# The first pair's quarter 12 and the sums s3 and s4 move to GpSimd

## The chip, the cores and the metric

One core of a Trainium2 chip. The metric is the device time of one execution in microseconds (us). Before the change three runs took 2365.22, 2365.63 and 2370.06 us; the median is 2365.63.

## The reference, cut to what matters

One step of a decoder layer for a prompt of 2048 tokens and for 8 samples of 8 tokens, with a model width of 1024. The part that the change touches comes first: the tokens are scaled and shifted by the conditioning vector, and then meet the large input projection.

```python
shift, scale, gate = jnp.split((jax.nn.silu(c) @ w_ada + b_ada)[:, None, :], 3, axis=-1)
h = x * (1 + scale) + shift
proj = h @ w_in
```

Everything that follows (windowed attention, a gated delta rule with its short convolution, two gated branches, an output projection and a layer norm) works on `proj` and is left as it is.

## The kernel before, in words

`modulate_and_project` computes `h` and `proj` with the tokens as the moving operand and the weights, two blocks of 128 output features at a time (a **pair**, counted by q), as the stationary one. There are two passes over the pairs: pass 0 for the first 1024 prompt tokens, pass 1 for the other 1024 and the samples.

Two schemes lie on top of each other. First, seven products stand for eight: the tokens of a pass are cut into four **quarters**, 11, 12, 21 and 22 (the first digit is the half of the tokens, the second the half of the 1024 features; a quarter is 128 partitions by 4 blocks of 512 tokens, so 128x2048), and the products are made of 11, 12, 22 and the sums s1 = 21 + 22, s2 = s1 - 11, s3 = 11 - 21, s4 = 12 - s2, with matching combinations of the weights. Second, each fp32 operand is split in two: a rounded high part (`m_hi` for tokens, `w_hi` for weights, written by ScalarE, line 447 or 423) and a **remainder** (`m_lo`, `w_lo`, written by VectorE as the operand less its high part, line 656 or 627). A product is then three matmuls for each of four blocks of the inner dimension: low by high, high by low, high by high (line 328).

The order of the first pair is written out by hand on each engine, and no planner moves anything:

- **SyncE** issues the loads in one queue: small ones, the first pair's weights, eight blocks of `w_ada`, then the quarters 11, 12, 21 into `x_half` and 22 into `m_sum` (line 243), then small ones and the weights of later pairs.
- **VectorE** (lines 828 to 845) modulates 11 in four pieces as soon as the shift and scale (`mods`, signal `mod_ready`) are there, makes 11's remainder in four pieces (831), modulates 21 (834), makes s3 (662), the remainder of 12 (656), s1, s2, the remainder of s1, s4, and the remainders of s2, 22, s4 and s3. Only then does it take up the results of the pair (`add`, 720) and the next pair's weights (`rest` 627; `weigh`, whose T1 is at line 635).
- **ScalarE** (from line 513) rounds the four pieces of 11 (523), modulates 12 (`modulated`, 439) and rounds it (`rounded`, 447), modulates 22, rounds s3, 22, s1 and s2, copies the first product out of PSUM (`copy_out`, 461), and rounds s4. Then the loop over the pairs starts: it splits the next pair's weights (`split`, 423) between the further copies; the split of form 2 waits for VectorE's T1, and the copy of the fourth product stands behind it.
- **TensorE** (`feature`, `product`) runs the products in the order 11, 12, s1, s2, 22, s4, s3. It waits for the remainder of each; for 11 alone block by block. Before "s2" it also needs the first copy, before "s4" the copy of "s1", and before "s3" that of "s2" (`f2_put`).
- **GpSimd** has no work there: it waits for results to store (lines 945 to 982). Later in the kernel it does have arithmetic: additions and subtractions of two tensors (lines 1612, 2384, 4048 to 4053), one scaling (1351) and memsets.

Of the kernel before, what the change touches and what calls it, by code (L numbers as in the profile page):

```python
# [9 lines left out]
ALU = mybir.AluOpType  # L10
ACT = mybir.ActivationFunctionType
# [4 lines left out]
KT = D // P  # L16
# [36 lines left out]
def f32(ap):  # L53

    return ap.bitcast(F32)
# [15 lines left out]
KH = KT // 2  # L71
PT = SEQ // 2
HT = PT // 2
# [20 lines left out]
def modulate_and_project(nc, t, sc, ab, g_last, head):  # L94
# [3 lines left out]
    with ExitStack() as ctx:  # L98
# [4 lines left out]
        m_hi, m_lo, m_sum = [None] * 7, [None] * 7, [None] * 7  # L103
# [9 lines left out]
        with ExitStack() as early:  # L113
            xs = sb("x_half", [P, 3, KH, WIDE], where=early)
# [29 lines left out]
        mods = sb("ada_mods", [P, 2 * KT, NC])  # L144
# [60 lines left out]
        def tokens(x, s):  # L205

            if s:
                return x[:, :, :]
            return x.rearrange("p k n -> p (k n)")[:, 0:KH * HT].rearrange("p (k n) -> p k n", n=HT)

        def slot(s, m):

            return AHEAD["21" if m == "21v" else m][s]
# [86 lines left out]
        def _(pe):  # L300
# [13 lines left out]
            def product(q, u, j, out, first, start):  # L314
                s = of_pass(q)
                at, n = UNITS[s][u]
                m, x = forms(s)[j]
                if u == 0:
                    pe.wait_ge(w_lo_done[j], q + 1)
                if first and (s, m) != (0, "11"):  # L320
                    pe.wait_ge(m_lo_done[s, m], 1)
                for k in range(KH):
                    if first and (s, m) == (0, "11"):
                        pe.wait_ge(m_lo_done[s, m], k + 1)
                    cols = slice(P * k, P * (k + 1))
                    hi, lo = tokens(m_hi[x], s)[:, k, at:at + n], tokens(m_lo[x], s)[:, k, at:at + n]
                    for nth, (l, r) in enumerate(((wh[j], lo), (wl[j], hi), (wh[j], hi))):
                        last = pe.matmul(out[:, 0:n], l[:, cols], r, start=start and k == 0 and nth == 0, stop=k == KH - 1 and nth == 2,  # L328
                                         skip_group_check=not start)
                last.then_inc(full[j], 1)  # L330
# [83 lines left out]
        def _(act):  # L414
# [18 lines left out]
            def modulated(s, m, x):  # L433
                key = (s, m)
                act.wait_ge(x_in[key], 16 * (1 + s))
                act.wait_ge(mod_ready, 2)
                for k in range(KH):
                    n = KH * (int(m[1]) - 1) + k
                    last = act.activation(x[:, k, 0:HT], x[:, k, 0:HT], ACT.Identity, scale=mods[:, KT + n, 0:1], bias=mods[:, n, 0:1])
                last.then_inc(x_mod[key], 1)  # L440

            def rounded(s, m, x, ready):

                n = HT + SS * s
                for sem_, count in ready:
                    act.wait_ge(sem_, count)
                act.activation(tokens(m_hi[slot(s, m)], s)[:, :, 0:n], x[:, :, 0:n], ACT.Copy).then_inc(m_hi_done[s, m], 1)
# [73 lines left out]
            for k in range(KH):  # L521
                act.wait_ge(x_mod[0, "11"], k + 1)
                act.activation(tokens(m_hi[0], 0)[:, k, :], a11[:, k, 0:HT], ACT.Copy).then_inc(m_hi_done[0, "11"], 1)
            modulated(0, "12", a12), rounded(0, "12", a12, [(x_mod[0, "12"], 1)])
            low = lambda s, m: tokens(m_sum[slot(s, m)], s)
            modulated(0, "22", low(0, "22"))
            rounded(0, "s3", low(0, "s3"), [(sum_put[0, "s3"], 1)])
            rounded(0, "22", low(0, "22"), [(x_mod[0, "22"], 1)])
            for m in ("s1", "s2"):
                rounded(0, m, low(0, m), [(sum_put[0, m], 1)])  # L530
            copy_out(0, 0, 0)
            rounded(0, "s4", low(0, "s4"), [(sum_put[0, "s4"], 1)])
            for q in range(NPAIR):
                nxt = q + 1 < NPAIR
                if q:
# [83 lines left out]
        def _(dve):  # L619
# [31 lines left out]
            def remainder(s, m, x):  # L651

                n = HT + SS * s
                dve.wait_ge(m_hi_done[s, m], 1)
                i = slot(s, m)
                put(dve.tensor_tensor(tokens(m_lo[i], s)[:, :, 0:n], x[:, :, 0:n], f32(tokens(m_hi[i], s)[:, :, 0:n]), ALU.subtract), m_lo_done[s, m])  # L656

            def combine(s, m, out, x, y, op, ready):
                n = HT + SS * s
                for sem_, count in ready:  # L660
                    dve.wait_ge(sem_, count)
                put(dve.tensor_tensor(out[:, :, 0:n], x[:, :, 0:n], y[:, :, 0:n], op), sum_put[s, m])
# [171 lines left out]
                last = dve.tensor_scalar(a21[:, k, 0:HT], a21[:, k, 0:HT], mods[:, KT + k, 0:1], mods[:, k, 0:1], ALU.mult, ALU.add)  # L834
            put(last, x_mod[0, "21"])
            s1, s2, s3, s4 = (low(0, m) for m in ("s1", "s2", "s3", "s4"))
            combine(0, "s3", s3, a11, a21, ALU.subtract, [(x_mod[0, "21"], 1), (x_mod[0, "11"], KH)])
            remainder(0, "12", a12)
            combine(0, "s1", s1, a21, a22, ALU.add, [(x_mod[0, "21"], 1), (x_mod[0, "22"], 1)])
            combine(0, "s2", s2, s1, a11, ALU.subtract, [(sum_put[0, "s1"], 1), (x_mod[0, "11"], KH)])  # L840
            remainder(0, "s1", s1)
            combine(0, "s4", s4, a12, s2, ALU.subtract, [(sum_put[0, "s2"], 1), (x_mod[0, "12"], 1)])
            remainder(0, "s2", s2), remainder(0, "22", a22), remainder(0, "s4", s4), remainder(0, "s3", s3)
            for b in range(4):
                dve.memset(stage[:, b, 0:S_PRE], 0.0)
            for q in range(NPAIR):
# [83 lines left out]
        @block.gpsimd  # L930
        def _(pool):
            def complete(q, j):

                if with_func(q):
                    pool.wait_ge(func_put, func_no(q, j) + 1)
                else:
                    pool.wait_ge((c21, c22)[j], units(q))
                    pool.wait_ge((c11, c12)[j], units(q))

            def store(q):  # L940
                s, n = of_pass(q), SPAN[of_pass(q)]
                dst = t[dict(q="q_d", k="k_T", z="z_d", g="g_d")[kind(q)]]
                for j in range(2):
                    complete(q, j)
                    pool.dma_start(dst[tile(q, j) - 2 * BASE[kind(q)], :, PT * s:PT * s + n],
                                   stage[:, buf(q, j), S_PRE:S_PRE + n]).then_inc(stored[buf(q, j)], 16)

            def store_tail(q):
                for j in range(2):
                    complete(q, j)  # L950
                    pool.dma_start(t["conv_tail"][tile(q, j)], stage[:, buf(q, j), PT:S_W]).then_inc(stored[buf(q, j)], 16)

            def store_conv(q):
                s, n = of_pass(q), SPAN[of_pass(q)]
                for j in range(2):
                    pool.wait_ge(conv_silu, conv_no(q, j) + 1)
                    pool.dma_start(t["conv_d"][tile(q, j), :, PT * s:PT * s + n], conv[:, j, 0:n]).then_inc(conv_stored[j], 16)  # L957

            def store_sums(q):
                s = of_pass(q)  # L960
                for j in range(2):
                    pool.wait_ge(sums_put, norm_pair(q) + 1)
                    row = t["norm_d"][tile(q, j):tile(q, j) + 1]
                    pool.dma_start(row[:, PT * s:PT * (s + 1)].rearrange("a (c n) -> (a c) n", n=HT),
                                   sums[2 * SUB * j:2 * SUB * (j + 1):SUB, :]).then_inc(sums_out, 16)
                    if s:
                        pool.dma_start(row[:, SEQ:], sums_s[SUB * j:SUB * j + 1, :]).then_inc(sums_out, 16)

            def store_all(q):
                if is_conv(q):  # L970
                    if of_pass(q):
                        store_tail(q)
                    store_conv(q)
                    if has_norm(q):
                        store_sums(q)
                else:
                    store(q)
            for q in range(NPAIR):
                store_all(q)
            for v, (s, g, b) in enumerate(VB):  # L980
                pool.wait_ge(v_read[v % 3], v // 3 + 1)
                pool.dma_start(t["v_out"][g, P * b:P * b + v_rows(b), :], v_sb[0:v_rows(b), v % VSLOTS, :]).then_inc(v_stored[v % VSLOTS], 16)
            for q in range(NPAIR, NQ - 1):
                store_all(q)
            for b in range(4):
                pool.wait_ge(stored[b], max(stores_to(q) for q in range(NQ - 1) if 2 * (q % 2) in (b, b - 1)))
            for j in range(2):
                pool.wait_ge(conv_stored[j], 16 * 2 * N_CONV)
            pool.wait_ge(sums_out, 16 * 3 * 2 * NHB)
            for j in range(VSLOTS):  # L990
                pool.wait_ge(v_stored[j], 16 * len(range(j, len(VB), VSLOTS)))
# [3257 lines left out]
```

## Time and profile before

| | us |
|---|---|
| median of three runs | 2365.63 |
| lowest and highest run | 2365.22, 2370.06 |
| the profiled execution, its own time | 2368.39 |
| its span, first to last instruction | 2366.6 |
| TensorE busy | 2255.3 (95% of the span) |
| VectorE busy | 1623.2 (69%) |
| ScalarE busy | 1169.0 (49%) |
| GpSimd busy | 374.4 (16%) |

The profile is of one execution. Times in it count from its first instruction. PE is TensorE's matmuls, PEld its weight loads, DVE is VectorE, ACT ScalarE, POOL GpSimd, SPq SyncE's queue. The mean granted TensorE clock is 0.978 of full speed. A row of an order of time reads: start in us, busy time in us, engine, line, operation, what is written from what is read, shape, number of instructions, and in brackets the idle time of the engine before it and what ended that.

### The profile page before, as it was taken

To read this page: it belongs to the slowest core of one execution; us is meant where nothing else is said; L and a number is where in the kernel's file an instruction comes from. 1 tells how busy PE (TensorE), PEld (TensorE's weight loads), DVE (VectorE), ACT (ScalarE), POOL (GpSimd) and SP (SyncE) were. 2 spreads that over 40 slices of the span, in tenths; PEclk is the share of its full clock that TensorE was granted. 3 is DMA by queue.
4 is the path that set the end of the run, shared out by engine and by line. 5 is a ranking of instruction groups with operands and counts; after the bars stand their busy time and mean duration, and the time that the engine had idled before them with its cause. 6 is when DMAs were issued, how large, how long until landed. Compare 5 with 4: busy or idle time off the path is not lost. (4 is left out here: it accounts for less than half of the span.)

```text
span 2366.6 us, 44948 instructions
## 1 busy us (share of the span) xinstructions
PE 2255.3 (95%) x16842; PEld 2027.6 (86%) x16842; DVE 1623.2 (69%) x3960; ACT 1169.0 (49%) x2457; POOL 374.4 (16%) x627
## 2 busy tenths in 40 slices
PE   5999999999999999999999999969998899999998
PEld 2778788888899999999999978658887689999786
DVE  5877776555363676776655558669986777778797
ACT  4444445444431454444444469647776533333554
POOL 0010100000111011110000001223321035445100
PEclk8999999999999999999999999989999699999999
DMA  7232323332532233223332368976565656666663
GB/s 272 98 116 98 116 99 116 107 107 89 197 116 75 94 105 122 82 109 112 112 109 81 126 235 281 323 218 170 149 185 181 193 172 213 194 206 233 199 208 125
DMA packets 256968, 363.55 MB, mean 154 GB/s; under 512 B 55654, under 2 KB 191438, under 8 KB 252272
## 3 DMA queue, kind: packets, MB, share of 16 engines
q1 hardware_dynamic: 197408, 224.24, 30.7%
q0 software_dynamic: 36496, 124.94, 13.8%
q10 hardware_dynamic: 22848, 11.50, 1.8%
q8 instruction: 134, 2.20, 0.4%
q14 instruction: 82, 0.67, 0.1%
HBM read 246.94 MB, written 113.68 MB: 152 GB/s over the span
## 5 line engine op out<-in xcount | busy, mean ns | idle before, releaser
L328 PE MATMUL ps_f<-m_lo,w_hi 128*128 128x272 f32 (+1 forms) x2436 | 787.8, 323 | 12.5 <-DVE m_lo L656 5.7
L328 PE MATMUL ps_f<-m_hi,w_lo 128*128 128x272 f32 (+1 forms) x2436 | 785.9, 323 | 0.0
L328 PE MATMUL ps_f<-m_hi,w_hi 128*128 128x272 f32 (+1 forms) x2436 | 784.5, 322 | 0.0
L328 PEld LDWEIGHTS ps_f<-m_lo,w_hi 128*128 128x128 f32 x2436 | 459.4, 189 | 52.7 <-issue 16.4
L328 PEld LDWEIGHTS ps_f<-m_hi,w_hi 128*128 128x128 f32 x2436 | 458.7, 188 | 32.2
L328 PEld LDWEIGHTS ps_f<-m_hi,w_lo 128*128 128x128 f32 x2436 | 459.2, 189 | 31.5
L720 DVE TENSOR_TENSOR stage<-partial,ps_f 128x512 f32<-128x512 f32 (+2 forms) x348 | 183.5, 544 | 303.6 <-PE ps_f L328 293.8
L461 ACT ACTIVATE partial<-ps_f 128x272 f32<-128x272 f32 (+1 forms) x348 | 161.2, 463 | 369.7 <-PE ps_f L328 368.7
L423 ACT ACTIVATE w_hi<-w_raw 128x512 fp32r<-128x512 f32 x348 | 213.0, 626 | 190.2 <-PE ps_f L328 110.6
L627 DVE TENSOR_TENSOR w_lo<-w_raw,w_hi 128x512 fp32r<-128x512 f32 x348 | 239.3, 688 | 82.9 <-ACT w_hi L423 78.9
L746 DVE SCALAR_TENSOR_TENSOR conv<-stage,side,conv 128x1024 f32<-128x1024 f32 x108 | 138.3, 1281 | 8.2 <-ACT conv L477 6.9
L66 PE MATMUL ps_f<-wv_lo,m_hi 128*128 128x256 f32 (+1 forms) x384 | 108.9, 284 | 3.7 <-DVE wv_lo L810 3.7
L67 PE MATMUL ps_f<-wv_hi,m_lo 128*128 128x256 f32 (+1 forms) x384 | 109.2, 284 | 0.0
L68 PE MATMUL ps_f<-wv_hi,m_hi 128*128 128x256 f32 (+1 forms) x384 | 108.9, 283 | 0.0
L67 PE MATMUL ps_fm<-u_hi,w_tail_lo 128*128 128x256 f32 (+1 forms) x336 | 95.6, 285 | 0.0
L67 PE MATMUL ps_fm<-u_first_hi,w_tail_lo 128*128 128x256 f32 x336 | 93.0, 277 | 0.0
L1480 ACT ACTIVATE probs<-probs,stats 128x128 f32<-128x128 f32 (+1 forms) x192 | 86.3, 454 | 10.5 <-DVE stats L1451 10.3
L957 POOL DMA_DIRECT2D scratch_conv_d<-conv x36 | 19.5, 540 | 427.5 <-ACT conv L483 420.8
L483 ACT ACTIVATE conv<-conv 128x1024 f32<-128x1024 f32 (+1 forms) x36 | 39.2, 1089 | 81.4 <-DVE conv L746 52.3
L66 PEld LDWEIGHTS ps_f<-wv_lo,m_hi 128*128 128x128 f32 x384 | 73.0, 190 | 4.1 <-DVE wv_lo L810 4.1
L1047 DVE TENSOR_TENSOR sub_prod<-sub_u,sub_w 96x60 f32<-96x60 f32 (+34 forms) x434 | 71.3, 203 | 4.0 <-issue 3.5
L68 PEld LDWEIGHTS ps_f<-wv_hi,m_hi 128*128 128x128 f32 x384 | 73.1, 190 | 0.0
(771 smaller groups left out, 4671.7 us busy)
## 6 DMA issues: line engine op xcount, KB each, us to landing
w_raw<-in_w_feat SPq DMA_DIRECT2D x58, 1024.0 KB, 5.7
gates<-scratch_g_d SPq DMA_DIRECT2D x56, 256.0 KB, 3.4
m_rows<-scratch_parts_d SPq DMA_DIRECT2D x16, 768.0 KB, 4.7
z_f<-scratch_z_d ACTq DMA_DIRECT2D x13, 768.0 KB, 6.8
scratch_conv_d<-conv POOLq DMA_DIRECT2D x18, 544.0 KB, 3.0
scratch_conv_d<-conv POOLq DMA_DIRECT2D x18, 512.0 KB, 2.9
kc<-in_k_cache SPq DMA_DIRECT2D x8, 1152.0 KB, 10.3
vc<-in_v_cache POOLq DMA_DIRECT2D x8, 1152.0 KB, 9.8
```

The lines of the kernel that those rows point to most:

```text
L66: pe.matmul(out, ah, bl, start=start, stop=False)
L67: pe.matmul(out, al, bh, start=False, stop=False)
L68: return pe.matmul(out, ah, bh, start=False, stop=stop)
L328: last = pe.matmul(out[:, 0:n], l[:, cols], r, start=start and k == 0 and nth == 0, stop=k == KH - 1 and nth == 2, skip_group_check=not start)
L423: act.activation(wh[j][:, :], source(q, j), ACT.Copy).then_inc(w_hi_done[j], 1)
L461: act.activation(f[:, which, 0:n], src[:, 0:n], ACT.Copy).then_inc(put, 1)
L483: act.activation(conv[:, j, 0:n], conv[:, j, 0:n], ACT.Silu).then_inc(conv_silu, 1)
L627: put(dve.tensor_tensor(wl[j][:, :], source(q, j), f32(wh[j][:, :]), ALU.subtract), w_lo_done[j])
L720: last = dve.tensor_tensor(by_residue(x[:, S_PRE:S_PRE + PT], stride_of(q), HT * h + at, m), left[:, 0:m], right[:, 0:m], ALU.add)
L746: put(dve.scalar_tensor_tensor(out=conv[:, j, 0:PT], in0=x[:, n:n + PT], scalar=w, in1=conv[:, j, 0:PT], op0=ALU.mult, op1=ALU.add), conv_ ...
L1047: dve.tensor_tensor(prod[:, rows, 0:m], u[:, i:i + 1, i + 1:].broadcast_to(some), w[:, rows, i:i + 1].broadcast_to(some), ALU.mult).then_i ...
L1480: act.activation(own, own, ACT.Exp, scale=-1.0, bias=stats[:, x.g, y.b, head:head + 1], accum_out=stats[:, x.g, y.b:y.b + 1, HPG + head]). ...
```

## The change

In pass 0's first pair, the quarter 12 is modulated by GpSimd, in four pieces that each give a signal, instead of by ScalarE. GpSimd also makes s3 and s4, which VectorE made. ScalarE modulates 22 directly after rounding 11, and then rounds 12 in four pieces, each with its signal; s3 is now rounded behind the first `copy_out`, just ahead of s4. VectorE makes 12's remainder in four pieces, and the remainder of 22 comes ahead of that of s2, with a wait for s4 between. TensorE's product of 12 waits block by block.

```diff
@@ product, TensorE
-                if first and (s, m) != (0, "11"):
+                if first and (s, m) not in ((0, "11"), (0, "12")):
                     pe.wait_ge(m_lo_done[s, m], 1)
                 for k in range(KH):
-                    if first and (s, m) == (0, "11"):
+                    if first and (s, m) in ((0, "11"), (0, "12")):
                         pe.wait_ge(m_lo_done[s, m], k + 1)
@@ ScalarE
-            modulated(0, "12", a12), rounded(0, "12", a12, [(x_mod[0, "12"], 1)])
             low = lambda s, m: tokens(m_sum[slot(s, m)], s)
             modulated(0, "22", low(0, "22"))
-            rounded(0, "s3", low(0, "s3"), [(sum_put[0, "s3"], 1)])
+            for k in range(KH):
+                act.wait_ge(x_mod[0, "12"], k + 1)
+                act.activation(tokens(m_hi[slot(0, "12")], 0)[:, k, :], a12[:, k, 0:HT], ACT.Copy).then_inc(m_hi_done[0, "12"], 1)
             rounded(0, "22", low(0, "22"), [(x_mod[0, "22"], 1)])
             for m in ("s1", "s2"):
                 rounded(0, m, low(0, m), [(sum_put[0, m], 1)])
             copy_out(0, 0, 0)
-            rounded(0, "s4", low(0, "s4"), [(sum_put[0, "s4"], 1)])
+            for m in ("s3", "s4"):
+                rounded(0, m, low(0, m), [(sum_put[0, m], 1)])
@@ VectorE
-            combine(0, "s3", s3, a11, a21, ALU.subtract, [(x_mod[0, "21"], 1), (x_mod[0, "11"], KH)])
-            remainder(0, "12", a12)
+            for k in range(KH):
+                dve.wait_ge(m_hi_done[0, "12"], k + 1)
+                i = slot(0, "12")
+                put(dve.tensor_tensor(tokens(m_lo[i], 0)[:, k, :], a12[:, k, 0:HT], f32(tokens(m_hi[i], 0)[:, k, :]), ALU.subtract), m_lo_done[0, "12"])
             combine(0, "s1", s1, a21, a22, ALU.add, [(x_mod[0, "21"], 1), (x_mod[0, "22"], 1)])
             combine(0, "s2", s2, s1, a11, ALU.subtract, [(sum_put[0, "s1"], 1), (x_mod[0, "11"], KH)])
-            remainder(0, "s1", s1)
-            combine(0, "s4", s4, a12, s2, ALU.subtract, [(sum_put[0, "s2"], 1), (x_mod[0, "12"], 1)])
-            remainder(0, "s2", s2), remainder(0, "22", a22), remainder(0, "s4", s4), remainder(0, "s3", s3)
+            remainder(0, "s1", s1), remainder(0, "22", a22)
+            dve.wait_ge(sum_put[0, "s4"], 1)
+            remainder(0, "s2", s2), remainder(0, "s4", s4), remainder(0, "s3", s3)
@@ GpSimd, ahead of its first store
+            low = lambda m: tokens(m_sum[slot(0, m)], 0)
+            a11, a12, a21 = (xs[:, n, :, 0:HT] for n in (1, 2, 0))
+            pool.wait_ge(x_in[0, "12"], 16)
+            pool.wait_ge(mod_ready, 2)
+            for k in range(KH):
+                n = KH + k
+                pool.tensor_scalar(a12[:, k, :], a12[:, k, :], mods[:, KT + n, 0:1], mods[:, n, 0:1], ALU.mult, ALU.add).then_inc(x_mod[0, "12"], 1)
+            pool.wait_ge(x_mod[0, "11"], KH)
+            pool.wait_ge(x_mod[0, "21"], 1)
+            pool.tensor_tensor(low("s3"), a11, a21, ALU.subtract).then_inc(sum_put[0, "s3"], 1)
+            pool.wait_ge(x_mod[0, "12"], KH)
+            pool.wait_ge(sum_put[0, "s2"], 1)
+            pool.tensor_tensor(low("s4"), a12, low("s2"), ALU.subtract).then_inc(sum_put[0, "s4"], 1)
```

## Rows read from the trace of the kernel before

**Rows 1.** Stretch, length, busy us (count) of PE, PEld, DVE, ACT, POOL; PEclk, DMA share, GB/s.

```profile
66.70:135.00 68.30, 68.26 (x307) 54.34 (x306) 52.81 (x73) 33.25 (x51) 6.70 (x12) 1.00 0.33 120
```

**Rows 2.** TensorE in order of time, the products that begin late, and "s2".

```profile
42.46 0.52 PE L328 MATMUL ps_f<-m_lo,w_hi 128*128 128x512 f32 x1 [2.91 <-DVE m_lo L656]
...
49.78 0.77 PE L328 MATMUL ps_f<-m_lo,w_hi 128*128 128x512 f32 x1 [2.74 <-DVE m_lo L656]
...
54.18 0.47 PE L328 MATMUL ps_f<-m_lo,w_hi 128*128 128x512 f32 x1
...
63.97 0.50 PE L328 MATMUL ps_f<-m_lo,w_hi 128*128 128x512 f32 x1 [1.38 <-ACT partial L461]
```

**Rows 3.** VectorE in order of time, the first pair.

```profile
33.34 2.50 DVE L831 TENSOR_TENSOR m_lo<-x_half,m_hi 128x512 fp32r<-128x512 f32 x4
35.87 1.92 DVE L834 TENSOR_SCALAR x_half<-x_half,ada_mods 128x512 f32<-128x512 f32 x4
...
40.03 2.29 DVE L656 TENSOR_TENSOR m_lo<-x_half,m_hi 128x2048 fp32r<-128x2048 f32 x1
...
51.75 8.89 DVE L656 TENSOR_TENSOR m_lo<-m_sum,m_hi 128x2048 fp32r<-128x2048 f32 x4
...
61.99 0.69 DVE L635 TENSOR_TENSOR w_raw<-w_raw 128x512 f32<-128x512 f32 x1
```

**Rows 4.** ScalarE in order of time: the modulations of 12 and 22, a copy.

```profile
34.20 2.93 ACT L439 ACTIVATE x_half<-x_half,ada_mods 128x512 f32<-128x512 f32 x4
...
38.97 2.93 ACT L439 ACTIVATE m_sum<-m_sum,ada_mods 128x512 f32<-128x512 f32 x4
...
63.33 0.58 ACT L461 ACTIVATE partial<-ps_f 128x512 f32<-128x512 f32 x1
```

**Rows 5.** Token loads: issues (min/median/max ns); issue of 22; us to landing, 12 then 22.

```profile
L243 SPq DMA_DIRECT2D x_half<-in_x_T x3: 448/6767/8660, 7.4 to 14.7; - x3
...
23.41 3.29 SPq L243 DMA_DIRECT2D m_sum<-in_x_T  x1
...
x_half<-in_x_T SPq DMA_DIRECT2D x1, 1024.0 KB, 25.2
...
m_sum<-in_x_T SPq DMA_DIRECT2D x1, 1024.0 KB, 15.3
```

**Rows 6.** GpSimd's arithmetic by line (ns min/median/max, first to last start); its memset.

```profile
L2384 POOL TENSOR_TENSOR ET_first<-G_first,causal_T x12: 1802/1816/1827, 1577.9 to 1737.6; 128x768 f32<-128x768 f32 x12
...
L4048 POOL TENSOR_TENSOR row_sums<-merged x32: 450/476/1442, 1898.3 to 2189.1; 128x128 f32<-128x128 f32 x32
...
L1351 POOL TENSOR_SCALAR q_bd_s<-q_s x12: 359/368/375, 1469.3 to 1473.7; 64x64 f32<-64x64 f32 x12
L1351 POOLq MODIFY_POOL_CONFIG  x2: 8/8/8, 1469.1 to 1469.2; - x2
...
1467.80 1.38 POOL L1344 MEMSET q_bd_s<- 128x1536 f32 x1 [101.25 <-PE ps_s L1380]
```

**Rows 7.** GpSimd and VectorE side by side in order of time; line 1047 by itself.

```profile
1674.25 3.58 POOL L2384 TENSOR_TENSOR ET_first<-G_first,causal_T 128x768 f32<-128x768 f32 x2
...
1676.70 1.18 DVE L1047 TENSOR_TENSOR sub_prod<-sub_u,sub_w 96x31 f32<-96x31 f32 x1
...
L1047 DVE TENSOR_TENSOR sub_prod<-sub_u,sub_w x9: 176/186/1181, 1676.7 to 1680.0; 96x29 f32<-96x29 f32 x2, 96x28 f32<-96x28 f32 x2, 96x31 f32<-96x31 f32 x1, 96x30 f32<-96x30 f32 x1
...
2168.63 0.80 POOL L4053 TENSOR_TENSOR row_sums<-merged,row_sums 128x128 f32<-128x128 f32 x1
2169.02 0.95 DVE L3731 TENSOR_TENSOR w_tail_lo<-x_res,w_hi_ahead 128x512 fp32r<-128x512 f32 x1
...
2169.89 0.68 DVE L3731 TENSOR_TENSOR w_tail_lo<-x_res,w_tail_lo 128x512 fp32r<-128x512 f32 x1
```

**Rows 8.** Busy time by stretch, columns as in the first group: around "s1" and "s2".

```profile
50.00:53.00 3.00, 3.00 (x8) 2.32 (x9) 3.00 (x2) 1.13 (x1) 0.00 (x0) 0.50 0.00 0
53.00:56.00 3.00, 3.00 (x14) 2.27 (x13) 3.00 (x2) 2.31 (x4) 0.00 (x0) 1.00 0.00 0
```

## The prediction

> **What bounds the kernel now.** The view of busy time by stretch comes first [rows 1]: from 66.7 us on TensorE is busy for 68.26 of 68.30 us. So TensorE is the bound behind the first pair, nothing there can win back lost time, and a shift of the first pair's last products goes into the span one for one. The question is only when the seven products of the first pair get their operands.
>
> TensorE's order of time [rows 2] shows where it stood idle: 2.91 us before the product of "12" (42.46), 2.74 us before "s1" (49.78), each until VectorE had a remainder, and 1.38 us before "s3" (63.97), until ScalarE had copied a product out. VectorE's order of time [rows 3] shows that it is the late one: from 33.34 to 60.64 (51.75 + 8.89) it works almost without a gap. A sum or remainder of 128x2048 takes 2.29 us and the next starts 2.2 us after it (8.89 less 2.29, over 3). "s2" started at 54.18, as its remainder came (51.75 + 2.29 = 54.04). From 54.18 to the end of "s4" at 62.59 (63.97 less the idle 1.38) TensorE ran through: 8.41 us for three products. The last wait hangs on VectorE too: ScalarE's copy at 63.33 [rows 4] stands behind the split that needs VectorE's weight difference of 61.99 [rows 3], so it comes 3.3 us (63.33 + 0.58 less 60.64) behind VectorE's last remainder.
>
> **What is removed.** VectorE loses s3 and s4, two instructions, 4.4 us of its chain. ScalarE loses four modulations, 2.93 us [rows 4], and gets four short roundings for a long one. The remainder of 12 becomes four pieces like those of 11, 2.5 us [rows 3] for 2.2: 0.3 more. The new waits on GpSimd stop nothing else of its own: all that is queued behind them there are stores of results of this pair and later ones, and those come after it. No DMA is moved or added, on no queue.
>
> **What is moved on ScalarE.** The modulation of 22 now stands ahead of the rounding of 12. The load of 22 is issued at 23.41 and lands 15.3 us later [rows 5], at 38.7; before, ScalarE came to it at 38.97 and waited for nothing. Now it is free at 34.2, stands until 38.7, modulates until 41.6 (2.93), and only then rounds 12, whose first piece is there at about 42.2. Before, 12's remainder started at 40.03. Passing 12 on in pieces gains nothing if they come this late.
>
> **What GpSimd costs.** The quarter 12 is issued at 7.85 (7.4 and the first issue's 0.45) and lands 25.2 us later [rows 5], at 33.1, so GpSimd starts there. Its two-input operations took 1.81 us for 768 elements and 0.47 for 128 [rows 6]: 2.09 ns for each further element, so some 0.2 fixed, and 4.5 us for the 2048 of s3 or s4, against VectorE's 2.29. Its one-input operation shows only at 64 elements, 0.37 us. For 512 the rows bound it: with the slope to the 1536-element memset (1.38 us, 0.69 ns an element) 0.68 us, with the two-input slope 1.31. I take 0.75, near the lower end, since one input is read.
>
> The first operation of that kind stands 0.1 to 0.2 us behind two MODIFY_POOL_CONFIG [rows 6], so I add nothing for it. The Trainium skill, "GPSIMD Engine Reference", section 2.1, says that the first call to a freshly loaded kernel pays for loading its code, about 6 us, with nothing in the profile to show it. By that the sum would be about 1.9 us longer (the third rival).
>
> **What both engines do to each other** decides. A VectorE operation of 96x31 with both inputs outside PSUM, 0.19 us elsewhere, took 1.18 us at 1676.70 [rows 7]: it ended at 1677.88, just behind the GpSimd pair that ended at 1677.83. So VectorE stands while GpSimd works, for the whole of a long operation. In the other direction GpSimd's 128-element operation took 0.80 between two of VectorE's, and VectorE's next took 0.95 instead of 0.68, 0.27 more, which is 128 times 2.09 ns: they take turns [rows 7]. All of VectorE's sums and remainders here are of that kind. So the 4.4 us taken from VectorE come back as two holds of some 4.4 us and four short ones.
>
> **The sum**, VectorE's chain step by step. The remainders of 11 ended at 35.84; four GpSimd modulations between them, 0.55 each (0.75 less the fixed 0.2), make it 38.0; the modulation of 21 (1.92; its data were there at 35.87 [rows 3]) 40.0. Then s3 runs on GpSimd from 40.1 to 44.6, and 12's first piece, ready at 42.2, waits: it ends the four at 47.1, 4.8 us later than before (42.3). s1 and s2: 51.5. Remainder of s1: 53.7 (before, its product could start at 49.78), its rounding in time at about 51.2. Now s4 has its turn and holds VectorE until 58.1. Remainder of 22: 60.3; of s2: 62.5; of s4: 64.7; of s3: 66.9, which is 6.3 us behind 60.64.
>
> On TensorE "12" starts at about 45.3, "s1" at 53.8, and "s2", whose remainder now stands behind that of 22, at 62.6 instead of 54.18. Three products of 8.41 us in all end at 71.0. The copy for "s3" is there at 66.9 + 3.3 = 70.2, so the 1.38 us of idle time are gone, and "s3" starts at 71.0 instead of 63.97: **7.0 us later**. The clock comes on top: after the idle time before "s1" the granted clock was 0.50 (the 1.2 GHz level) in 50 to 53 us, with 8 matmuls against 14 in the next 3 us at 1.00 (2.4 GHz) [rows 8]. There the slow stretch lay before a wait; now a longer idle time, about 5 us, lies just ahead of "s2", and nothing behind it waits. Six matmuls at 0.227 us (2.72 a product of 12) are 1.4 us. Sum: 8.4 us later.
>
> The profiled execution took 2368.39 us (span 2366.6), so it would be 2376.8. It lies 2.8 us above the median of the runs, 2365.63; on the median the sum gives **2374.0**. A change under 0.2%, 4.7 us, is about what a measurement of this kernel can't tell from none.
>
> **Rivals.** (1) GpSimd holds VectorE up little or not at all over a long operation. Then the remainder of 12 still waits for ScalarE: pieces from 42.2, end at 44.5, s1 and s2 at 48.9, remainder of s1 51.1, of 22 53.4, of s2 55.6 (s4 ready at 53.5). "s2" starts 1.5 us later than before and "s4" ends at 64.1 instead of 62.59, which the 1.38 us of idle time swallow: "s3" starts at about 64.1, within 0.2 us of before, so no change, 2365.8; with half the holds, about 4 us. Against it: [rows 7]. Chance 0.24.
>
> (2) It turns out faster: neither holds nor the wait for 22 bite, because 22 lands in time. Then VectorE is short of 4.4 us: the remainder of 12 ends at 40.3, s2 at 44.7, the remainder of s2, behind that of 22 and GpSimd's s4 (49.2), at 51.4, "s2" starts at 51.5, 2.7 us earlier, "s4" ends at 59.9, and "s3" starts 4.1 us earlier: 2361.5. It decides from a landing of 22 before about 35 us on, and [rows 5] put it at 38.7. Chance 0.06, only half of it over 0.2%.
>
> (3) GpSimd's first modulation starts about 6 us late. Then it falls on 39.1 to 42.5; the remainders of 11 are not disturbed, but s3 runs from 42.6 to 47.1 across 12's pieces, which end at 49.0 instead of 47.1: 1.9 us more than the sum, 10.3 later, 2375.9. For it: nothing in the rows; this kernel has one such first use, without a gap. Chance 0.08.
>
> **How the numbers follow.** My forecast has 0.62. With the modulations at 1.31 us instead of 0.75 it is 2.2 us more; without a slow stretch 1.4 less, with one twice as long 1.4 more. The range reaches from rival 1, a little above no change, to the sum with rival 3 and a longer slow stretch: 2366 to 2378. Slower by over 0.2%: forecast, rival 3 and a little of rival 1, 0.74. Within 0.2%: 0.23. Faster: 0.03.
>
> **What would show it.** Right: VectorE rows in the first 70 us stretched to 4 us and more where s3 and s4 run; ScalarE idle until 38.7 for 22's load; "s2" starting near 62 to 64 us and "s3" at 71 to 73. Wrong: sums and remainders still 2.29 us beside a busy GpSimd, or "s3" before 64 us.

## The result, and the profile after

| | before | after |
|---|---|---|
| median, us | 2367.38 (9 runs, 2364.64 to 2374.61) | 2375.47 (9 runs, 2373.43 to 2381.21) |
| ratio to before, 95% interval | | 1.0035 [1.0025, 1.0044] |
| span of the profiled execution | 2366.6 | 2373.5 |
| mean granted TensorE clock | 0.978 | 0.975 |
| busy: VectorE, ScalarE, GpSimd | 1623.2, 1169.0, 374.4 | 1625.8, 1164.2, 390.1 |

The changed kernel is 0.35% slower, 8.3 us on 2367.38 by the ratio and 8.1 by the difference of the medians; all of the interval lies above the 0.2% that the prediction named. The predicted 2374.0 stood on a median of 2365.63, so the predicted difference was 8.4.

VectorE lost two instructions of 2.29 us and is busier all the same. The page of the changed kernel, busy us with share of the span and number of instructions:

```profile
PE 2260.9 (95%) x16842; PEld 2032.1 (86%) x16842; DVE 1625.8 (68%) x3961; ACT 1164.2 (49%) x2456; POOL 390.1 (16%) x633
```

**Where it happens.** VectorE's order of time in the first pair, changed kernel (it answers to [rows 3]; 11's modulation began at 31.30 here, at 31.52 before):

```profile
33.13 2.49 DVE L833 TENSOR_TENSOR m_lo<-x_half,m_hi 128x512 fp32r<-128x512 f32 x4
35.78 3.50 DVE L836 TENSOR_SCALAR x_half<-x_half,ada_mods 128x512 f32<-128x512 f32 x4 [0.16 <-DMA x_half<-in_x_T]
42.14 4.16 DVE L842 TENSOR_TENSOR m_lo<-x_half,m_hi 128x512 fp32r<-128x512 f32 x4 [2.86 <-ACT m_hi L528]
46.22 2.28 DVE L664 TENSOR_TENSOR m_sum<-x_half,m_sum 128x2048 f32<-128x2048 f32 x1
48.53 2.29 DVE L664 TENSOR_TENSOR m_sum<-m_sum,x_half 128x2048 f32<-128x2048 f32 x1
50.74 15.49 DVE L658 TENSOR_TENSOR m_lo<-m_sum,m_hi 128x2048 fp32r<-128x2048 f32 x5
67.58 0.69 DVE L637 TENSOR_TENSOR w_raw<-w_raw 128x512 f32<-128x512 f32 x1
```

GpSimd's order of time in the same stretch:

```profile
33.14 5.86 POOL L988 TENSOR_SCALAR x_half<-x_half,ada_mods 128x512 f32<-128x512 f32 x4 [32.69 <-DMA x_half<-in_x_T]
39.43 4.52 POOL L991 TENSOR_TENSOR m_sum<-x_half 128x2048 f32<-128x2048 f32 x1 [0.43 <-DVE x_half L836]
50.97 6.51 POOL L994 TENSOR_TENSOR m_sum<-x_half,m_sum 128x2048 f32<-128x2048 f32 x1 [7.03 <-DVE m_sum L664]
```

The order of time adds up neighbours of one line. The view of one line or tile has the single durations of the changed kernel (ns, min/median/max, then first to last start); here VectorE's remainders of the sums, its modulation of 21, its remainder of 12, and GpSimd's modulation of 12:

```profile
L658 DVE TENSOR_TENSOR m_lo<-m_sum,m_hi x5: 2277/2278/6683, 50.7 to 64.0; 128x2048 fp32r<-128x2048 f32 x5
...
L836 DVE TENSOR_SCALAR x_half<-x_half,ada_mods x4: 760/992/993, 35.8 to 38.3; 128x512 f32<-128x512 f32 x4
...
L842 DVE TENSOR_TENSOR m_lo<-x_half,m_hi x4: 676/678/2348, 42.1 to 45.6; 128x512 fp32r<-128x512 f32 x4
...
L988 POOL TENSOR_SCALAR x_half<-x_half,ada_mods x4: 921/928/3117, 33.1 to 38.1; 128x512 f32<-128x512 f32 x4
```

The first two of the five remainders, each from an order of time over a window that lies inside it, that of s1 and that of 22:

```profile
50.74 2.28 DVE L658 TENSOR_TENSOR m_lo<-m_sum,m_hi 128x2048 fp32r<-128x2048 f32 x1
...
52.94 6.68 DVE L658 TENSOR_TENSOR m_lo<-m_sum,m_hi 128x2048 fp32r<-128x2048 f32 x1
```

Read the two engines against each other. The remainder of s1 began at 50.74, 0.23 us ahead of GpSimd's s4 (50.97), and took 2.28 us as before. Then s4 had its turn: it ended at 57.48 (50.97 + 6.51), and its record is 2.0 us longer than that of s3, because it stood until the remainder of s1 was over. VectorE's next instruction, the remainder of 22, began at 52.94 and took 6.68 us instead of 2.28: it stood until s4 was over and ended at 59.62. The three behind it take 2.28 again. So one instruction that takes GpSimd 4.5 us by itself (s3, 4.52) was paid by VectorE with 4.40 us. The same at 42.14: the first piece of 12's remainder takes 2.35 us instead of 0.68 and ends at 44.49, behind the end of s3 on GpSimd (43.95). And 21's modulation takes 3.50 us instead of 1.92, taking turns with three of GpSimd's pieces.

**What it does to TensorE.** Its order of time, changed kernel, first matmul of "12", "s1", "s2" and "s3" (answers to [rows 2]):

```profile
44.64 0.77 PE L328 MATMUL ps_f<-m_lo,w_hi 128*128 128x512 f32 x1 [5.35 <-DVE m_lo L842]
...
53.17 0.77 PE L328 MATMUL ps_f<-m_lo,w_hi 128*128 128x512 f32 x1 [3.41 <-DVE m_lo L658]
...
61.98 0.77 PE L328 MATMUL ps_f<-m_lo,w_hi 128*128 128x512 f32 x1 [4.47 <-DVE m_lo L658]
...
72.25 0.39 PE L328 MATMUL ps_f<-m_lo,w_hi 128*128 128x512 f32 x1
```

Busy time by stretch of the changed kernel, columns as in [rows 1]:

```profile
58.00:62.00 4.00, 0.02 (x1) 0.05 (x1) 4.00 (x3) 2.94 (x4) 0.00 (x0) 0.68 0.00 0
62.00:66.00 4.00, 4.00 (x10) 3.14 (x11) 4.00 (x2) 0.00 (x0) 0.00 (x0) 0.50 0.02 4
66.00:70.00 4.00, 4.00 (x19) 3.30 (x18) 3.90 (x11) 1.12 (x2) 0.00 (x0) 0.96 0.01 2
70.00:72.30 2.30, 2.30 (x12) 1.91 (x11) 2.04 (x4) 1.49 (x3) 0.00 (x0) 1.00 0.00 0
66.70:135.00 68.30, 68.30 (x306) 55.63 (x305) 53.58 (x76) 34.28 (x52) 4.52 (x8) 1.00 0.26 93
```

"s2" starts 7.80 us later than before. In front of it TensorE stood for 4.47 us (busy for 0.02 us from 58 to 62, while the granted clock fell to a mean of 0.68), and behind that it ran at 0.50, the 1.2 GHz level, from 62 to 66 us: 10 matmuls in 4 us, against 19 in the next 4. "s3" starts at 72.25, 8.28 later, with no idle time in front. From the first matmul of "s2" (61.98) to the last of "s4" (72.03) it is 10.05 us, where before it was 8.02 (54.18 to 62.20): 2.0 for the clock. From 66.7 us on nothing is idle. ScalarE's order of time, changed kernel: the modulation of 22, the copy that "s3" needs, and the one that answers to a copy at 121.04 us before, well behind the first pair:

```profile
38.66 2.93 ACT L439 ACTIVATE m_sum<-m_sum,ada_mods 128x512 f32<-128x512 f32 x4 [4.59 <-DMA m_sum<-in_x_T]
...
68.93 0.58 ACT L461 ACTIVATE partial<-ps_f 128x512 f32<-128x512 f32 x1
...
128.85 0.58 ACT L461 ACTIVATE partial<-ps_f 128x512 f32<-128x512 f32 x1
```

The last row gives the measure that is used from here on. 128.85 - 121.04 = 7.81; 11's modulation began 0.22 earlier (the loads in front of it vary), so the first pair has become **8.03 us** longer. "s3" itself is 8.50 later on the same start; "s3" to that copy has become 0.5 us shorter, since TensorE now runs through. Before, it had stood ahead of "s3", whose second matmul came 0.33 us behind the first instead of 0.23, and it stood again in the second pair, where the matmul of 83.33 came 0.42 behind the one before it and the next 0.34 behind that. The profiled spans differ by 6.9 alone; one execution of each can't say more, since the span wanders behind the first stages: in the fifth run below that stretch is as before within 0.1 us, and its span is 2362.7 against 2366.6.

### The profile page after: what moved, and what is told of

It reads as the page before. It is cut to its first block and busy times, and to the rows that moved or that the text cites. A ratio compares the mean times of both kernels' runs of the same rounds, so it can differ in the third digit from the quotient of the medians.

```text
span 2373.5 us, 44955 instructions
## 1 busy us (share of the span) xinstructions
PE 2260.9 (95%) x16842; PEld 2032.1 (86%) x16842; DVE 1625.8 (68%) x3961; ACT 1164.2 (49%) x2456; POOL 390.1 (16%) x633
```

## The experiments

The theories, with the letters of the expectations. **H**, the prediction's: VectorE stands for as long as GpSimd reads beside it, so what GpSimd takes over comes back as holds. **Q**: the order on ScalarE costs the time, since 12 is rounded only behind the wait for 22. **D**: VectorE is not held; it only gets its data late. **F**: GpSimd's first operation is late. The table has what is read from every run: start of 11's modulation, end of VectorE's last remainder of the first pair, the length of that chain, the copy that answers to the one at 121.04 us, and its shift less the shift of the start. Each ratio is to executions of the kernel before that were made beside the run; their medians were 2367.38 for the changed kernel, 2367.3 for runs 1 to 3, 2367.13 for runs 4 to 6 and 2368.39 for run 8, so a ratio isn't the quotient of two medians of this table.

| run | start | end | chain | copy | shift | median, us | ratio to before [95%] |
|---|---|---|---|---|---|---|---|
| before | 31.52 | 60.64 | 29.12 | 121.04 | | 2367.38 | |
| after | 31.30 | 66.24 | 34.94 | 128.85 | +8.0 | 2375.47 | 1.0035 [1.0025, 1.0044] |
| 1, 12 rounded first | 30.84 | 65.79 | 34.95 | 129.24 | +8.9 | 2377.42 | 1.0045 [1.0029, 1.006] |
| 2, sums on VectorE | 30.79 | 62.41 | 31.62 | 123.21 | +2.9 | 2370.65 | 1.0013 [0.9997, 1.0029] |
| 3, s2 ahead of 22 | 32.25 | 67.20 | 34.95 | 127.57 | +5.8 | 2375.95 | 1.0034 [1.0019, 1.0049] |
| 4, idle reads | 32.29 | 67.26 | 34.97 | 127.61 | +5.8 | 2374.11 | 1.0023 [1.0012, 1.0035] |
| 5, idle memsets | 32.07 | 61.16 | 29.09 | 121.52 | -0.1 | 2366.27 | 0.9994 [0.998, 1.0007] |
| 6, copy first | 31.72 | 60.20 | 28.48 | 120.57 | -0.7 | 2367.91 | 1.0002 [0.9991, 1.0013] |
| 7, small scaling first | 30.79 | 66.00 | 35.21 | 129.45 | +9.1 | 2372.98 | a single run |
| 8, copy first in two pairs | 31.44 | 59.96 | 28.52 | 118.34 | -2.6 | 2366.32 | 0.9991 [0.998, 1.0001] |

### 1: the changed kernel, with 12 rounded ahead of the modulation of 22

```diff
-            modulated(0, "22", low(0, "22"))
             for k in range(KH):
                 act.wait_ge(x_mod[0, "12"], k + 1)
                 act.activation(...)
+            modulated(0, "22", low(0, "22"))
```

> The changed kernel with one edit: ScalarE rounds the four pieces of 12 before it modulates 22, not after. Theory H (GpSimd and VectorE hold each other up): the pieces are rounded by about 39.6 instead of 43.7, but s3 on GpSimd (4.5 us from about 39.4) still falls among VectorE's pieces of 12, so VectorE's four pieces end at 46 as now (46.3), "s2" starts at 61.5 to 62.5 and the time is within 1 us of the changed kernel's. Rival Q (ScalarE's wait for the load of 22 is what costs): 12's remainder is done at about 42, everything behind it comes 3 to 4 us earlier, "s2" near 58, and the kernel is 3 to 4 us faster than the changed one.

VectorE's order of time in this run:

```profile
39.06 6.82 DVE L842 TENSOR_TENSOR m_lo<-x_half,m_hi 128x512 fp32r<-128x512 f32 x4
```

TensorE's, "12" and its second block, and "s2":

```profile
39.89 0.47 PE L328 MATMUL ps_f<-m_lo,w_hi 128*128 128x512 f32 x1 [1.84 <-DVE m_lo L842]
44.74 0.80 PE L328 MATMUL ps_f<-m_lo,w_hi 128*128 128x512 f32 x1 [3.58 <-DVE m_lo L842]
...
61.54 0.76 PE L328 MATMUL ps_f<-m_lo,w_hi 128*128 128x512 f32 x1 [3.66 <-DVE m_lo L658]
```

The wait for 22 no longer stands in front of 12, and "12" starts 4.75 us earlier (4.3 on the same start). It does no good: s3 runs on GpSimd from 39.29 for 4.85 us, the four remainders of 12 take 6.82 us instead of 2.5, and TensorE stands behind the first block. The chain is 34.95 us, as in the changed kernel. The wait for 22 and the hold by s3 lie in the same time; taking the first away lengthens the second. The time is not shorter either (1.0045 against 1.0035). Q falls: as long as s3 runs on GpSimd, the wait for 22 costs nothing of its own.

### 2: the changed kernel, with both sums back on VectorE

```diff
+            combine(0, "s3", s3, a11, a21, ALU.subtract, [...])
             for k in range(KH):          # remainder of 12, in pieces
...
-            remainder(0, "s1", s1), remainder(0, "22", a22)
-            dve.wait_ge(sum_put[0, "s4"], 1)
-            remainder(0, "s2", s2), remainder(0, "s4", s4), remainder(0, "s3", s3)
+            remainder(0, "s1", s1)
+            combine(0, "s4", s4, a12, s2, ALU.subtract, [...])
+            remainder(0, "s2", s2), remainder(0, "22", a22), remainder(0, "s4", s4), remainder(0, "s3", s3)
@@ GpSimd
-            pool.tensor_tensor(low("s3"), a11, a21, ALU.subtract).then_inc(sum_put[0, "s3"], 1)
-            pool.tensor_tensor(low("s4"), a12, low("s2"), ALU.subtract).then_inc(sum_put[0, "s4"], 1)
```

> The changed kernel with s3 and s4 made by VectorE again, at their old places, and the old order of the remainders; GpSimd keeps the modulation of 12, ScalarE its new order, 12 its pieces. Theory H: two holds of some 4.4 us go, two instructions of 2.2 us come back; from the changed kernel's rows VectorE's last remainder ends at about 62 instead of 66.2, "s2" starts at 55.5 to 56 instead of 62.0, "s3" at 65 to 66 instead of 72.3: 6 to 7 us faster than the changed kernel and 1 to 2 us slower than the one before (2368 to 2370 where before is 2367). Rival Q: ScalarE's wait for 22's load is still there, so the time stays within 1 us of the changed kernel's 2375.

VectorE's order of time: s3, the remainder of 12, and the last four remainders:

```profile
39.12 2.29 DVE L664 TENSOR_TENSOR m_sum<-x_half 128x2048 f32<-128x2048 f32 x1
42.18 2.50 DVE L843 TENSOR_TENSOR m_lo<-x_half,m_hi 128x512 fp32r<-128x512 f32 x4 [0.77 <-ACT m_hi L528]
...
53.52 8.89 DVE L658 TENSOR_TENSOR m_lo<-m_sum,m_hi 128x2048 fp32r<-128x2048 f32 x4
```

With two instructions more, VectorE ends 3.3 us sooner (chain 31.62 for 34.94), and none of these rows is longer than before. Of the 8.0 us, 5.1 go with the sums and the order of the remainders that went with them. The 2.9 that stay are 12 on GpSimd, which lengthens 21's modulation, and the wait for 22, which shows as 0.77 us in front of 12; no run divides them between the two. They are a little too many: 12's remainder starts at 42.18 here and at 42.14 in the changed kernel, since both wait for the landing of 22, though this run's start is 0.51 us earlier. On the changed kernel's start the 2.9 would be some 2.4, an estimate. Its time lies between before and after; the interval takes in no change.

### 3: the changed kernel, with the remainder of s2 again ahead of that of 22

```diff
-            remainder(0, "s1", s1), remainder(0, "22", a22)
+            remainder(0, "s1", s1)
             dve.wait_ge(sum_put[0, "s4"], 1)
-            remainder(0, "s2", s2), remainder(0, "s4", s4), remainder(0, "s3", s3)
+            remainder(0, "s2", s2), remainder(0, "22", a22), remainder(0, "s4", s4), remainder(0, "s3", s3)
```

> The changed kernel with the remainder of s2 ahead of that of 22 again (both behind the wait for s4). Theory O (putting 22 first costs one instruction of 2.2 us before "s2"): GpSimd's s4 holds VectorE in any case, so "s2" starts at about 59.8 instead of 62.0, "s3" at about 70 instead of 72.3, 2 us faster; VectorE's last remainder still ends at 66.2. Rival: the order is free, because "s3" waits in the end for VectorE's last remainder and the copy behind it; then "s3" stays at 72 and the time within 0.5 us of the changed kernel's.

VectorE's order of time in this run, where the remainder of s2 now waits for s4:

```profile
58.30 8.90 DVE L658 TENSOR_TENSOR m_lo<-m_sum,m_hi 128x2048 fp32r<-128x2048 f32 x4 [4.47 <-POOL m_sum L994]
```

TensorE's, the first matmul of "s2":

```profile
60.73 0.47 PE L328 MATMUL ps_f<-m_lo,w_hi 128*128 128x512 f32 x1 [2.19 <-DVE m_lo L658]
```

On the changed kernel's start (31.30 for 32.25) that is 59.78, 2.2 us before its 61.98, one remainder; at 121 us the shift is 5.8 instead of 8.0. The chain has its length still: as a wait or as a hold, VectorE pays s4 in full. The times of this run don't tell it from the changed kernel (1.0034 against 1.0035, with an interval of 0.15% to either side), so the 2.2 us stand on the traces.

### 4 and 5: the kernel before, with idle work on GpSimd that nobody needs

Everything is computed as before. In run 4 GpSimd subtracts two quarters twice, 1536 elements each, into a tile that isn't in use yet; in run 5 it writes zeros there instead, two memsets in each place. No engine gets data from it; the waits that guard the tile were over long before they were reached.

```diff
+            a11, a21, to = xs[:, 1, 0:3, 0:HT], xs[:, 0, 0:3, 0:HT], f[:, 1:4, :]
+            pool.wait_ge(x_mod[0, "11"], KH)
+            pool.wait_ge(x_mod[0, "21"], 1)
+            pool.tensor_tensor(to, a11, a21, ALU.subtract).then_inc(idle_put, 1)   # run 5: two pool.memset(to, 0.0)
+            pool.wait_ge(sum_put[0, "s2"], 1)
+            pool.wait_ge(idle_put, 1)
+            pool.tensor_tensor(to, a11, a21, ALU.subtract).then_inc(idle_put, 1)   # run 5: two pool.memset(to, 0.0)
```

> The kernel before, with everything in its place, and two GpSimd subtractions of 128x1536 added whose result nobody uses (inputs 11 and 21, output a place that is free until the second copy): one when 21 is modulated, one when s2 is there. Nothing waits for them but writes that come after 54 us, long behind them. Theory H: each holds VectorE for some 3.2 us (1536 times 2.09 ns), so VectorE's last remainder ends at 66 to 67 instead of 60.6, "s2" starts at 60 to 61 instead of 54.2, "s3" at 69 to 71 instead of 64.0, and the kernel is 5 to 7 us slower than before. Rival D (the change is slow by its new order and waits alone): no row of VectorE is longer than 2.3 us, and the time is that of the kernel before within 1 us.

> The kernel before with four GpSimd memsets of 128x1536 instead of the two subtractions, two at each of the same places, so 5.5 us of GpSimd work that reads nothing. Theory H in the form that only reading GpSimd work holds VectorE: VectorE's last remainder ends at 60.6 to 61, the time is that of before within 1 us. Rival (any GpSimd work holds VectorE): the last remainder ends 4 to 5.5 us later, and the kernel is 4 to 5 us slower.

Run 4, VectorE in order of time: the remainder of 12, s4, and the last four remainders:

```profile
40.68 5.53 DVE L658 TENSOR_TENSOR m_lo<-x_half,m_hi 128x2048 fp32r<-128x2048 f32 x1
...
52.86 5.59 DVE L664 TENSOR_TENSOR m_sum<-x_half,m_sum 128x2048 f32<-128x2048 f32 x1
58.37 8.89 DVE L658 TENSOR_TENSOR m_lo<-m_sum,m_hi 128x2048 fp32r<-128x2048 f32 x4
```

Run 4, GpSimd in order of time:

```profile
38.59 5.46 POOL L984 TENSOR_TENSOR partial<-x_half 128x1536 f32<-128x1536 f32 x1 [38.14 <-DVE x_half L836]
50.82 5.48 POOL L987 TENSOR_TENSOR partial<-x_half 128x1536 f32<-128x1536 f32 x1 [6.76 <-DVE m_sum L664]
```

Run 5, VectorE in order of time, s3, the remainder of 12 and that of s1:

```profile
38.25 2.29 DVE L664 TENSOR_TENSOR m_sum<-x_half 128x2048 f32<-128x2048 f32 x1
40.46 2.28 DVE L658 TENSOR_TENSOR m_lo<-x_half,m_hi 128x2048 fp32r<-128x2048 f32 x1
...
47.85 2.29 DVE L658 TENSOR_TENSOR m_lo<-m_sum,m_hi 128x2048 fp32r<-128x2048 f32 x1 [0.58 <-ACT m_hi L448]
```

Run 5, GpSimd in order of time, its first two memsets and the third:

```profile
38.34 1.38 POOL L984 MEMSET partial<- 128x1536 f32 x1 [37.89 <-DVE x_half L836]
39.78 1.38 POOL L986 MEMSET partial<- 128x1536 f32 x1
...
47.33 1.38 POOL L989 MEMSET partial<- 128x1536 f32 x1 [6.17 <-DVE m_sum L664]
```

This pair decides between H and D. In run 4 nobody waits for GpSimd, and still one VectorE instruction beside each idle one is longer by 3.24 and 3.30 us, which is 1536 times the 2.09 ns that the prediction worked out from [rows 6], 3.2. The chain grows by 5.85 us and the kernel by 0.23%. Note the place: GpSimd's first one starts at 38.59, while VectorE makes s3, loses about 2 us to it, and then it is the instruction behind s3 that stands, as with s4 in the changed kernel. In run 5 GpSimd is at work in the same places, and no VectorE row is longer than 2.29. So it is not work as such that holds VectorE but work that reads. The Trainium skill, "SBUF — State Buffer", section "Who interferes with whom", says just this: a VectorE instruction with two inputs in SBUF contends with a GpSimd instruction that reads SBUF, and not with one that only writes it. Both halves agree with these rows.

### 6 and 8: the kernel before, with a copy ahead of the split

The idle 1.38 us before "s3" [rows 2] stand in the kernel before too. In run 6 ScalarE rounds 22 behind the first copy, and in the first pair makes the copy of the second result ahead of the second split; in run 8 it does the latter in the second pair as well.

```diff
-            rounded(0, "22", low(0, "22"), [(x_mod[0, "22"], 1)])
...
             copy_out(0, 0, 0)
+            rounded(0, "22", low(0, "22"), [(x_mod[0, "22"], 1)])
...
+                if q == 0:               # run 8: q < 2
+                    copy_out(q, 0, 1)
...
-                copy_out(q, 0, 1)
+                if q:                    # run 8: q >= 2
+                    copy_out(q, 0, 1)
```

> The kernel before without GpSimd's help, with two moves on ScalarE: the copy that "s3" waits for comes ahead of the split that waits for VectorE's weight difference, and the rounding of 22 comes behind those of s1 and s2. If the chain of the first pair is read rightly, the idle 0.5 us before s1's remainder and the idle 1.4 us before "s3" go: "s3" starts at 61.9 to 62.6 instead of 64.0 and the kernel is 1.4 to 2 us faster than before, 0.06 to 0.09%, which the times may not show and the trace must. Rival: "s3" starts no earlier, because another wait is right behind.

> The kernel with the copy first, and the same move in the second pair too: there the copy stood behind a SiLU that waits for VectorE's convolution, and TensorE was idle for 1.69 us at 82.88. If that is the whole of the new wait, TensorE has no gap over 1 us between "s1" of the first pair and 135 us, and the products behind 120 us come 2 to 2.5 us earlier than in the kernel before; over the span that is 0.1%, within what the times can tell. Rival: VectorE is the bound through the second pair as well, and a third wait takes the place of the second, so that they come less than 1 us earlier.

Run 6, TensorE in order of time, its only idle time between "s3" and 135 us:

```profile
82.88 0.50 PE L328 MATMUL ps_f<-m_lo,w_hi 128*128 128x512 f32 x1 [1.69 <-ACT partial L461]
```

Run 8, busy time by stretch, columns as in [rows 1]:

```profile
66.70:135.00 68.30, 68.30 (x308) 54.68 (x308) 53.71 (x75) 33.68 (x51) 6.70 (x12) 1.00 0.34 124
```

Run 6 takes the wait of 1.38 us away ("s3" starts at 61.99, as expected) and has a new one of 1.69 us in the second pair, where the same copy stands behind the same split; 0.7 us are left. Run 8 takes that one away too, and by the trace the copy at 118.34 is 2.6 us earlier than before. The times don't confirm it: 0.9991, with 1.0001 inside the interval. It is the lowest ratio of these runs, and no version was found that is faster by more than the measurement can tell.

### 7: the changed kernel, with a small scaling as GpSimd's first

GpSimd scales 128x16 elements into a tile not in use yet as soon as `mods` is there, before 12 has landed.

```diff
             pool.wait_ge(mod_ready, 2)
+            pool.tensor_scalar(f[:, 3, 0:2 * KT], mods[:, :, 0:1], mods[:, 0, 0:1], mods[:, KT, 0:1], ALU.mult, ALU.add).then_inc(warm, 1)
+            pool.wait_ge(x_in[0, "12"], 16)
```

> The changed kernel, and GpSimd does one scaling of 16 elements (its result is used by nobody) between the signal that the shift and scale are there and the landing of 12. In the changed kernel the first modulation of 12 on GpSimd took 3.1 us, the others 0.93. Theory F (the first operation of a kind is slow by itself, some 2 us): now the small one takes 2 us or more and the first modulation of 12 is down to 1 to 1.5 us, and it comes between VectorE's remainders of 11. Theory H (it stood behind VectorE's four remainders of 11, which ended at 35.6): the small one takes under 0.6 us, or waits for VectorE's modulation of 11, and the first modulation of 12 still ends at about 36.3.

GpSimd in order of time:

```profile
30.86 0.63 POOL L987 TENSOR_SCALAR partial<-ada_mods 128x16 f32<-128x16 f32 x1 [30.41 <-DVE ada_mods L827]
```

Its modulations of 12 in the view of their line (ns, min/median/max):

```profile
L991 POOL TENSOR_SCALAR x_half<-x_half,ada_mods x4: 767/928/2607, 33.1 to 37.4; 128x512 f32<-128x512 f32 x4
```

In the changed kernel the first of GpSimd's four modulations took 3.12 us, the others 0.93. If that had been the price of a first use, it would sit on the small operation here. That one took 0.63 us (H had put it under 0.6), and the first modulation still took 2.61. What both have in common is its end: 36.25 in the changed kernel, 35.76 here, each time some 0.65 us behind VectorE's last remainder of 11 (33.13 + 2.49 = 35.62 and about 35.1). In run 3, where VectorE came to these remainders later and ended them at 36.57, it took 3.77 us and ended at 37.05. So it is held, and F falls. How a first use is set up can be seen in the changed kernel's view of GpSimd's line, on its queue:

```profile
L988 POOLq MODIFY_POOL_CONFIG  x2: 8/10/11, 1.4 to 1.4; - x2
```

It stands 32 us ahead of the first use, where before it was at 1469.1 us, directly ahead of the only one [rows 6].

## Why the prediction was right, step by step

- **ScalarE's wait for 22**: 38.66 (predicted 38.7), and 12's first remainder starts at 42.14 (42.2). Read from the landing in [rows 5] alone.
- **GpSimd's two sums**: 4.52 us for s3 (4.5), worked out from the lengths at 128 and 768 elements. s3 ran from 39.43 to 43.95 (40.1 to 44.6).
- **GpSimd's modulations**: this step failed, at no cost to the sum. The prediction put four holds of 0.55 us between the remainders of 11. They were undisturbed (2.49 us), GpSimd got no turn among them, and took its turns with the modulation of 21 instead, which became 1.58 us longer; predicted were 2.2. At the end of 21's modulation the forecast was 40.0 and the run 39.28. The prediction had left a modulation of one input out of the holds altogether; pieces of 0.99 us, 0.54 before, show that it belongs there.
- **12's pieces** end at 46.30 (47.1), s1 and s2 at 50.82 (51.5).
- **The hold by s4**: 4.40 us (4.4), and in the place that the prediction gave it, behind the remainder of s1 (53.02, predicted 53.7) and on that of 22. VectorE's last remainder ends at 66.24 (66.9).
- **TensorE**: "12" at 44.64 (45.3), "s1" at 53.17 (53.8), "s2" at 61.98 (62.6); the idle time before "s3" is gone, as said.
- **The clock** was undersized: 2.0 us measured and 1.4 predicted. The slow stretch was to last six matmuls; ten lie in 62 to 66 us. The 8.41 us for the three products were 0.16 too many, since they run to the end of the last matmul, and "s3" can start before that (8.25 by the starts).
- **Behind the first pair** nothing was to be won back; of the 8.5 us at "s3", on the same start, 0.5 was.
- **Sum**: 8.4 us predicted, 8.03 in the trace, 8.3 by the ratio. On the same start "s2" came 0.4 us sooner than forecast, the clock cost 0.6 more and 0.5 was won back, so the misses of size cancel for the larger part. That the number is this near is partly luck; that s3 and s4 would hold VectorE, and where, is not.

Rival 1 (no hold, or half) is refuted by runs 4 and 2, in both signs. Rival 2 (22 lands early) is refuted by the 38.66. Rival 3 (GpSimd's first modulation six us late) did not come to pass: it began at 33.14, as its data landed, and run 7 shows what made it long. The rule behind it (the Trainium skill, "GPSIMD Engine Reference", section 2.1: the first call to a freshly loaded kernel pays some 6 us) shows in no row: if there was such a load, it ended in the time that GpSimd stood idle before 30.9 us.

The runs divide the 8.0 us so: 2.9 stay without the sums on GpSimd (run 2), 2.9 more come with the sums (run 3 less run 2, both with s2 ahead of 22), and 2.2 more with 22 ahead of s2 (after less run 3). Runs 1 and 7, whose chains are within 0.3 us of the changed kernel's, have shifts of 8.9 and 9.1, so each of these parts is good to about 1 us. What differs there is the clock: "s3" starts 11.1 us behind "s2" in both, 10.27 in the changed kernel and 9.9 in run 3, for the same 36 matmuls. Busy time by stretch, the changed kernel and then run 1, columns as in [rows 1]:

```profile
66.00:68.00 2.00, 2.00 (x10) 1.65 (x9) 1.90 (x8) 0.00 (x0) 0.00 (x0) 0.92 0.00 0
...
66.00:68.00 2.00, 2.00 (x7) 1.58 (x6) 1.90 (x4) 0.05 (x1) 0.00 (x0) 0.60 0.00 0
```

So the term for the clock is not a fixed price: from 1.7 us in run 3 to 2.9 in runs 1 and 7 (9.9 and 11.1 less 8.25).

## What to carry to other kernels

An instruction that goes from VectorE to GpSimd is not gone from VectorE if it reads SBUF beside instructions with two SBUF inputs: here it came back as a hold of GpSimd's full working time (4.40 us for 2048 elements, 3.24 and 3.30 for 1536), nearly twice the 2.29 us saved. Count it on VectorE, and put such work beside instructions that it doesn't hold; GpSimd's memsets cost VectorE nothing (run 5). Before an order in a queue is changed, look up when each load lands: here one row told to 0.1 us how long ScalarE would stand. And removing one wait shows the next (run 6), so a gain is read at a point well behind it.

## What the runs showed of the hardware that was not expected

GpSimd doesn't always get a turn. Between VectorE's four remainders of 11, which follow each other without a gap, it got none: in the changed kernel and in run 7 its first modulation stood until the last of them was over (3.12 and 2.61 us for 0.93). Beside three of the four pieces of 21's modulation the two took turns, 0.99 us a piece on VectorE (0.54 before) and 0.93 on GpSimd, and of long instructions each let the other in once: the remainder of s1, then s4, then the remainder of 22. That VectorE's modulation is held at all, with one large input, agrees with the Trainium skill, "SBUF — State Buffer", section "Who interferes with whom", which has tensor_scalar among the operations that can enter a mode that takes the shared ports; that one of two engines is shut out over four instructions is read from these rows alone. The kind of instruction differs (two inputs, then one), but no run here varied it alone, so why one is shut out and the other takes turns stays open. Run 3 adds two rows to it. There GpSimd's first modulation began at 33.29, while 11's modulation still ran, and the last piece of that, 0.33 us later, took its usual 0.55; so one input alone gave no turn at that place. And 21's modulation followed the remainders without a gap, and GpSimd's turn came there all the same; so a gap on VectorE isn't needed. What moves the span behind the first stages by several us between executions stays open too.
